# The gain of the first norm as one row, spread by TensorE, and transposes of the identity while the head waits

## The chip, the cores and the metric

The kernel runs on one core of a Trainium2 chip. The metric is the device time of one execution in microseconds; the median of several runs counts. The engines are PE (TensorE, matrix products and transposes), DVE (VectorE), ACT (ScalarE), POOL (GpSimd) and SP (SyncE, which here issues all the loads and stores). Each engine works through its own queue in order, and waits on semaphores for the others.

## What is computed

One step of a hybrid encoder layer on 1024 prompt rows and 32 sample rows of width 1024, all in f32: an RMS norm, one input projection whose columns feed window attention and a gated MLP over positions, an output projection with a residual, a second RMS norm with a SwiGLU of inner width 2816, a residual, and a last RMS norm. The part that matters here is the start:

```python
def rms_norm(x, g, eps=1e-6):
    xf = x.astype(jnp.float32)
    y = xf * lax.rsqrt(jnp.mean(xf * xf, axis=-1, keepdims=True) + eps)
    return (y * g.astype(jnp.float32)).astype(x.dtype)
...
        hp = rms_norm(yp, g_mix[l])
        q, k, v, u, g = project(hp, w_in[l])
```

`g_mix` is a vector of 1024 values, the gain of the first norm; every row of x is multiplied by it, element by element.

## The kernel before

The 1056 rows are nine tiles: eight of 128 rows and one of 32 (the sample). The head turns each tile into the form that the projection reads. `norm_front(r)` is shared by three engines: ACT squares the tile and sums it along the row (line 1530), POOL makes the root (lines 955 and 958), and DVE multiplies the tile by that root and by the gain in one instruction, `scalar_tensor_tensor` (line 1925), into `xn`. `norm_back(r)` follows: PE transposes `xn` in eight blocks of 128x128 against the identity `ident` into two banks of PSUM (line 1145), ACT rounds the result to the high part of `h_first`, `h_mid` or `h_late` (line 1537), and DVE subtracts it from the unrounded values for the low part (line 1905, the helper `low`). `split(n)` does the same with a 128-column unit of weights, ACT on line 1547 and DVE in `low`. `proj_block(n, half)` then multiplies: for each of eight k it makes three products (`three_passes`, lines 1108 to 1110) of 384 columns (288 for the last three tiles); a half is four k, twelve products. The first block needs the low parts of tiles 0, 1 and 2 and the first unit of weights.

The order of all this is written out by hand. `make_schedule()` gives one list, and PE, ACT, DVE and POOL each walk through it and do what concerns them:

```python
    s = [("front", 0), ("front", 1), ("back", 0), ("front", 2), ("split", 0), ("back", 1),
         ("front", 3), ("back", 2), ("split", 1), ("front", 4), ("back", 3), ("front", 5),
         ("block", 0, 0), ("back", 4), ("front", 6), ("block", 0, 1), ("back", 5), ("front", 7),
```

SP issues the loads in an order of its own (line 662 on): tile 0, the gain, tiles 1 and 2, the first weights. The gain is read from HBM 128 times, once for each partition:

```python
            load_rows(0)
            sp.dma_start(gain[:, :], a["g_mix"][0].partition_broadcast(P)).then_inc(gain_landed, 16)
            load_rows(1)
            load_rows(2)
```

The same tile `gain` later holds `g_ffn` and `g_final`, loaded in the same way. PSUM has eight banks of 128x512 f32, `ps[:, 0..7, :]`: the projection goes round banks 0 to 3, the transposes of the head use banks 4 to 7. POOL makes the constants at the start (lines 936 to 943), the identity last; `pool_consts` counts them. `one_row` is a row of ones on one partition, used by the attention for a mask.

Of the kernel before, what the change touches and what calls it, by code (L numbers as in the profile page):

```python
# [11 lines left out]
P = 128  # L12
# [252 lines left out]
def build(nc, a, o):  # L265
# [3 lines left out]
    with ExitStack() as ctx:  # L269
# [35 lines left out]
        one_row = sb("one_row", [1, DH])  # L305
# [117 lines left out]
        gain_landed = sem("gain_landed")  # L423
        wsp_landed = sem("wsp_landed")
# [189 lines left out]
        def _(sp):  # L614
# [46 lines left out]

            load_rows(0)
            sp.dma_start(gain[:, :], a["g_mix"][0].partition_broadcast(P)).then_inc(gain_landed, 16)
# [437 lines left out]
        def _(pe):  # L1101
# [23 lines left out]

            def norm_back(r):

                i = tile_of(r)
                rows, n = row_parts(i), (P if i != SAMPLE else DEC)
                pe.wait_ge(xn_ready, r + 1)  # L1130
                if r == 0:
                    pe.wait_ge(pool_consts, 6)
                if 2 <= r < ROWS:
                    pe.wait_ge(lo_ready, r - 1)
                if r == ROWS:
                    pe.wait_ge(attn_ready, UNITS)
                if r >= ROWS + 2:

                    pe.wait_ge(plain_lo, r - ROWS - 1)
                    if (r - ROWS) % 2 == 1:  # L1140
                        pe.wait_ge(t_2_ready, (r - ROWS) // 2)
                out = turned_pair(r)
                src = xn[rows, i % 2, :] if r < ROWS else xn_ffn[rows, :]
                for k in range(KT):
                    t = turn(out[:, k, 0:n], src[:, P * k:P * k + P], ident[rows, rows])  # L1145
                t.then_inc(turned, 1)

            def proj_block(n, half):
                t, b = PROJ_BLOCKS[n]
                if half != 1:  # L1150
                    if b == 0:
                        pe.wait_ge(split_lo, PLACE[t] + 1)
# [61 lines left out]
            def scores(u):  # L1214
# [7 lines left out]
                for x, i in enumerate(rows):  # L1222
                    for h in range(2):
# [13 lines left out]
                        if i == 0:  # L1237
                            mm(out[0:DH, at + DH:at + P], neg_row[:, :], one_row[:, :], start=True, stop=True)
                        else:
                            mm(out[0:DH, at + DH:at + P], q, k_t[hp, even - DH:even], start=True, stop=True)  # L1240
# [71 lines left out]

            for item in SCHEDULE:
# [186 lines left out]
        def _(act):  # L1500
# [31 lines left out]

            def norm_back(r):
# [71 lines left out]
            for item in SCHEDULE:  # L1605
# [3 lines left out]
                elif kind == "back":  # L1609
                    norm_back(item[1])  # L1610
                elif kind == "split":
# [291 lines left out]
        def _(dve):  # L1903
# [12 lines left out]
            def norm_front(r):  # L1916
# [4 lines left out]
                if r % ROWS == 0:  # L1921
# [4 lines left out]
                                               in1=gain[rows, :], op0=ALU.mult,  # L1926
# [511 lines left out]
```

## Time and profile before

| | us |
|---|---|
| median of 3 runs | 1028.12 (1028.02 to 1028.37) |
| the profiled execution | 1028.31 |
| its span | 1026.6 |
| PE busy | 1004.0 (98%) |
| DVE busy | 626.5 (61%) |
| ACT busy | 389.2 (38%) |
| POOL busy | 411.8 (40%) |

The span runs from the first to the last instruction that the profiler saw; 1.7 us of the execution's time lie around it. PE's share of busy time is close to the whole, but its products overlap by design, so their busy time doesn't tell how fast they follow each other: for that one reads the starts. All times in the rows below count from the start of the span.

### The profile page before, as it was taken

The numbers are of one execution on the slowest core, as the hardware profiler recorded it, in microseconds if no ns is written. First come the engines' busy times: TensorE is split into PE (matmuls) and PEld (weight loads), VectorE is DVE, ScalarE is ACT, GpSimd is POOL, SyncE is SP. The second block draws the span as 40 slices with busy tenths as digits, with TensorE's granted clock in tenths as the row PEclk, the third lists the DMA queues.
The fourth block names the chain that finished last, engine by engine and source line by source line (L and its number), as shares of the span: only waits on it lengthen the run. The fifth ranks groups of instructions, "written<-read, shape, count | busy, mean of one in ns | idle before, by whom it ended". The sixth has DMA issues, their size and how long they took to land.

```text
span 1026.6 us, 16280 instructions
## 1 busy us (share of the span) xinstructions
PE 1004.0 (98%) x5754; PEld 835.9 (81%) x5754; DVE 626.5 (61%) x877; ACT 389.2 (38%) x701; POOL 411.8 (40%) x444
## 2 busy tenths in 40 slices
PE   5999999999999999999999999999999999999997
PEld 4999998888887887787787787877878777877786
DVE  5475636766245786676766667666764737635725
ACT  6411145445232543333333333333333446324431
POOL 2011100000000467696696786876974400202045
PEclk9999999999999999999999999999999999999999
DMA  8311331100321444453643643644637999478814
GB/s 281 100 45 43 85 86 43 43 2 1 123 103 67 149 113 145 146 178 108 180 151 113 194 148 108 203 134 135 184 109 230 307 343 387 173 283 311 307 41 169
DMA packets 166274, 155.84 MB, mean 152 GB/s; under 512 B 16240, under 2 KB 129296, under 8 KB 166224
## 3 DMA queue, kind: packets, MB, share of 16 engines
q1 hardware_dynamic: 166224, 155.16, 47.0%
q8 instruction: 33, 0.54, 0.2%
q14 instruction: 17, 0.14, 0.0%
HBM read 114.17 MB, written 41.06 MB: 151 GB/s over the span
## 4 chain that ended last, share of the span: by engine, by line
PE 85%; DMA 6%; DVE 5%; SPq 1%; ACT 1%; issue 1%; POOL 0%; POOLq 0%; DVEq 0%; ACTq 0%
PE ps L1108 26%; PE ps L1110 25%; PE ps L1109 25%; DMA xd_in<-act_scratch 3%; PE ps L1394 2%; PE ps L1145 1%; DMA act_scratch<-act_sums 1%; PE ps L1280 1%; PE ps L1258 1%; DMA out_state_gmlp_v_sample<-work 1%; DVE x_dn L1905 1%; PE ps L1242 1%; DMA act_scratch<-ffn_blocks_even 1%; DVE work L1990 1%; PE ps L1482 1%
## 5 line engine op out<-in xcount | busy, mean ns | idle before, releaser
L1108 PE MATMUL ps<-x_forms,w_forms 128*128 128x512 f32 (+1 forms) x644 | 246.2, 382 | 0.7 <-DVE w_forms L1905 0.7
L1109 PE MATMUL ps<-x_forms,w_forms 128*128 128x512 f32 (+1 forms) x644 | 244.7, 380 | 0.0
L1110 PE MATMUL ps<-x_forms,w_forms 128*128 128x512 f32 (+1 forms) x644 | 244.5, 380 | 0.0
L1108 PEld LDWEIGHTS ps<-x_forms,w_forms 128*128 128x128 f32 x644 | 121.1, 188 | 28.2 <-issue 4.7
L1110 PEld LDWEIGHTS ps<-x_forms,w_forms 128*128 128x128 f32 x644 | 121.1, 188 | 23.0
L1109 PEld LDWEIGHTS ps<-x_forms,w_forms 128*128 128x128 f32 x644 | 121.1, 188 | 22.6
L1108 PE MATMUL ps<-w_dn,x_dn 128*128 128x512 f32 x308 | 121.6, 395 | 1.1 <-DVE y_acc_sample L2368 1.1
L1110 PE MATMUL ps<-w_dn,x_dn 128*128 128x512 f32 x308 | 119.9, 389 | 0.0
L1109 PE MATMUL ps<-w_dn,x_dn 128*128 128x512 f32 x308 | 119.9, 389 | 0.0
L955 POOL TENSOR_SCALAR meansq<-sumsq 128x1 f32<-128x1 f32 (+1 forms) x26 | 9.5, 365 | 246.3 <-ACT xn_ffn L1530 223.1
L1689 ACT CAST w_forms<-w_sums 128x512 fp32r<-128x512 f32 x88 | 54.6, 623 | 109.9 <-PE ps L1110 104.2
L1905 DVE TENSOR_TENSOR w_dn<-wd_in,w_dn 128x1024 fp32r<-128x1024 f32 (+1 forms) x42 | 49.3, 1174 | 73.3 <-ACT w_dn L1820 72.0
L1905 DVE TENSOR_TENSOR w_forms<-w_sums,w_forms 128x512 fp32r<-128x512 f32 x88 | 72.0, 829 | 18.9 <-ACT w_forms L1689 18.8
L1108 PEld LDWEIGHTS ps<-w_dn,x_dn 128*128 128x128 f32 x308 | 57.8, 188 | 23.5 <-issue 6.7
L1820 ACT CAST w_dn<-wd_in 128x1024 fp32r<-128x1024 f32 (+1 forms) x42 | 41.1, 978 | 90.5 <-DMA wd_in<-in_w_down 42.0
L1110 PEld LDWEIGHTS ps<-w_dn,x_dn 128*128 128x128 f32 x308 | 57.8, 188 | 12.2
L1109 PEld LDWEIGHTS ps<-w_dn,x_dn 128*128 128x128 f32 x308 | 57.8, 188 | 11.6
L1905 DVE TENSOR_TENSOR x_dn<-xd_in,x_dn 128x1024 fp32r<-128x1024 f32 (+1 forms) x42 | 51.7, 1230 | 6.4 <-ACT x_dn L1833 4.4
L1069 POOL TENSOR_TENSOR y_acc_even<-resid,down_u 128x512 f32<-128x512 f32 x4 | 6.2, 1560 | 106.0 <-DVE down_u L2345 78.3
L2212 DVE TENSOR_TENSOR ffn_q<-ffn_q 128x512 f32<-128x512 f32 (+1 forms) x23 | 19.8, 860 | 46.0 <-ACT ffn_q L1708 46.0
L1833 ACT CAST x_dn<-xd_in 128x1024 fp32r<-128x1024 f32 (+1 forms) x42 | 41.2, 980 | 11.7 <-DMA xd_in<-act_scratch 11.6
L1905 DVE TENSOR_TENSOR wbuf<-stage,wbuf 128x1024 fp32r<-128x1024 f32 x22 | 26.8, 1219 | 29.2 <-ACT wbuf L1547 29.2
(254 smaller groups left out, 2113.0 us busy)
## 6 DMA issues: line engine op xcount, KB each, us to landing
xd_in<-act_scratch SPq DMA_DIRECT2D x35, 512.0 KB, 7.3
t_raw<-in_w_down SPq DMA_DIRECT2D x88, 128.0 KB, 2.6
act_scratch<-act_sums SPq DMA_DIRECT2D x22, 512.0 KB, 4.5
y_acc_odd<-in_w_down SPq DMA_DIRECT2D x22, 512.0 KB, 6.4
wd_in<-t_scratch SPq DMA_DIRECT2D x20, 512.0 KB, 7.0
wd_in<-in_w_down SPq DMA_DIRECT2D x15, 512.0 KB, 6.5
stage<-in_w_in SPq DMA_DIRECT2D x28, 256.0 KB, 3.5
w_stage_even<-in_w_gate SPq DMA_DIRECT2D x22, 256.0 KB, 3.3
```

Source lines behind the costliest of these rows:

```text
L1108: mm(out, wh, xh, start=first, stop=False, skip_group_check=onto)
L1109: mm(out, wh, xl, start=False, stop=False, skip_group_check=onto)
L1110: return mm(out, wl, xh, start=False, stop=last, skip_group_check=onto)
L1145: t = turn(out[:, k, 0:n], src[:, P * k:P * k + P], ident[rows, rows])
L1242: last = mm(out[DH:P, at:at + P], cat[hp, j, odd:odd + DH], k_t[hp, even:even + P], start=True, stop=True)
L1258: t = turn(ps[:, 6, at:at + P], probs[:, u % 3, 2 * h + x, :], ident[:, :])
L1394: t = mm(out, x_sample[:, k, :], w_stage[q][:, :, k, :], start=k < 4, stop=k >= KT - 4)
L1689: nc.scalar.copy(wf[:, n, 0, :, :], src).then_inc(w_form_hi, 1)
L1820: nc.scalar.copy(w_dn[k % RING][:, 0, 0:pairs, :], wd_in[k % STAGED_FORMS][:, 0:pairs, :]).then_inc(w_dn_hi, 1)
L1833: nc.scalar.copy(x_dn[k % RING][:, 0, 0:pairs, :], xd_in[k % STAGED_FORMS][:, 0:pairs, :]).then_inc(x_dn_hi, 1)
L1905: return nc.vector.tensor_tensor(out, x, hi.bitcast(F32), ALU.subtract)
L2212: nc.vector.tensor_tensor(pq[:, 0, cols], pq[:, 0, cols], pq[:, 1, cols], ALU.add).then_inc(q_ready, 1)
```

## The change

The gain of the first norm is no longer loaded 128 times. SP loads it once, as its first load, into partition 0 of `gain`. PE, ahead of everything else in its queue, multiplies a row of ones (`one_row`, now 128 long) with it in two products of 512 columns (`spread_gain`), which leaves the gain on all partitions of PSUM banks 2 and 3. DVE's products of tiles 0, 1 and 2 read it there. After `norm_back(1)` ACT has a new step, `keep_gain`: it waits until DVE has made tile 2 and copies the gain from PSUM into `gain`, from where DVE reads it from tile 3 on. The block that goes to bank 2 first waits for that copy.

Besides, PE transposes the identity into bank 1, with no reader (`idle_turns`): 14 times before `norm_back(0)`, 8 times each before `norm_back(1)` and `norm_back(2)`, in each case ahead of the wait for the tile, and 6 times before the first block, ahead of its waits.

```diff
-        one_row = sb("one_row", [1, DH])
+        one_row = sb("one_row", [1, P])
...
+            sp.dma_start(gain[0:1, :], a["g_mix"][0:1, :]).then_inc(gain_landed, 16)
             load_rows(0)
-            sp.dma_start(gain[:, :], a["g_mix"][0].partition_broadcast(P)).then_inc(gain_landed, 16)
             load_rows(1)
...
+            def spread_gain():
+
+                pe.wait_ge(pool_consts, 6)
+                pe.wait_ge(gain_landed, 16)
+                for h in range(2):
+                    t = mm(ps[:, 2 + h, :], one_row[:, :], gain[0:1, 512 * h:512 * h + 512], start=True, stop=True)
+                t.then_inc(gain_spread, 1)
+
+            def idle_turns(n):
+
+                for _ in range(n):
+                    turn(ps[:, 1, 0:P], ident[:, :], ident[:, :])
...
             def norm_back(r):
...
+                if r < 3:
+                    idle_turns([14, 8, 8][r])
                 pe.wait_ge(xn_ready, r + 1)
-                if r == 0:
-                    pe.wait_ge(pool_consts, 6)
...
             def proj_block(n, half):
                 t, b = PROJ_BLOCKS[n]
                 if half != 1:
+                    if n == 0:
+                        idle_turns(6)
+                    if n == 2:
+                        pe.wait_ge(gain_kept, 1)
...
+            spread_gain()
             for item in SCHEDULE:
...
+            def keep_gain():
+                act.wait_ge(xn_ready, 3)
+                nc.scalar.copy(gain[:, :], ps[:, 2:4, :].rearrange("p b c -> p (b c)")).then_inc(gain_kept, 1)
...
                     norm_back(item[1])
+                    if item[1] == 1:
+                        keep_gain()
...
-                if r % ROWS == 0:
+                g = gain[rows, :]
+                if r == 0:
+                    dve.wait_ge(gain_spread, 1)
+                if r < 3:
+                    g = ps[:, 2:4, :].rearrange("p b c -> p (b c)")
+                elif r == 3:
+                    dve.wait_ge(gain_kept, 1)
+                elif r % ROWS == 0:
                     dve.wait_ge(gain_landed, 16 * (r // ROWS + 1))
...
-                                               in1=gain[rows, :], op0=ALU.mult,
+                                               in1=g, op0=ALU.mult,
```

PE's queue at its start, before: the transposes of four tiles (32 of 128x128), then the first products of the projection.

```order
1 L1145 MATMUL ps<-ident,work 128x128 x32
2 L1108 MATMUL ps<-h_first,wbuf 128x384
3 L1109 MATMUL ps<-h_first,wbuf 128x384
4 L1110 MATMUL ps<-h_first,wbuf 128x384
5 L1108 MATMUL ps<-h_first,wbuf 128x384
```

The same place in the changed kernel: line 1133 is `spread_gain`, line 1139 the transposes of the identity, line 1160 those of the tiles, lines 1110 to 1112 the products of the projection.

```order
1 L1133 MATMUL ps<-gain,one_row 128x512 x2
2 L1139 MATMUL ps<-ident 128x128 x14
3 L1160 MATMUL ps<-ident,work 128x128 x8
4 L1139 MATMUL ps<-ident 128x128 x8
5 L1160 MATMUL ps<-ident,work 128x128 x8
6 L1139 MATMUL ps<-ident 128x128 x8
7 L1160 MATMUL ps<-ident,work 128x128 x16
8 L1139 MATMUL ps<-ident 128x128 x6
9 L1110 MATMUL ps<-h_first,wbuf 128x384
```

Tiles 2 and 3 follow each other with nothing between them, and the last six stand behind tile 3.

ACT's queue at its start, before: the squares (line 1530), the casts of tiles 0, 1, 2 (line 1537) and of weights (line 1547).

```order
2 L1530 ACTIVATE work,sumsq<-work 128x1024 x2
3 L1537 CAST h_first<-ps 128x8x128
4 L1530 ACTIVATE work,sumsq<-work 128x1024
5 L1547 CAST wbuf<-stage 128x1024
6 L1537 CAST h_first<-ps 128x8x128
7 L1530 ACTIVATE work,sumsq<-work 128x1024
8 L1537 CAST h_first<-ps 128x8x128
```

And in the changed kernel, where squares are on line 1550, casts on lines 1561 and 1571, and the copy of the gain on line 1555.

```order
2 L1550 ACTIVATE work,sumsq<-work 128x1024 x2
3 L1561 CAST h_first<-ps 128x8x128
4 L1550 ACTIVATE work,sumsq<-work 128x1024
5 L1571 CAST wbuf<-stage 128x1024
6 L1561 CAST h_first<-ps 128x8x128
7 L1555 COPY gain<-ps 128x1024
8 L1550 ACTIVATE work,sumsq<-work 128x1024
9 L1561 CAST h_first<-ps 128x8x128
```

The copy stands between the cast of tile 1 and the square of tile 3.

## Rows read from the trace of the kernel before

**Rows 1.** The page: the span, and each engine's busy time, share and instructions.

```profile
span 1026.6 us, 16280 instructions
...
PE 1004.0 (98%) x5754; PEld 835.9 (81%) x5754; DVE 626.5 (61%) x877; ACT 389.2 (38%) x701; POOL 411.8 (40%) x444
```

**Rows 2.** Waits of PE over the whole span: total us, times, longest us.

```profile
PE ps L1145 <- DVE work L1925: 11.9, 4, 7.9
PE ps L1255 <- DVE work L2068: 1.3, 1, 1.3
```

**Rows 3.** Chain that ended last, its first microseconds: start us, us, what.

```profile
0.81 0.39 SPq L660
1.25 5.30 DMA gain<-in_g_mix
```

**Rows 4.** PE's timeline of the head: start us, us, engine, line, op, out<-in, shapes.

```profile
7.92 1.97 PE L1145 MATMUL ps<-ident,work 128*128 128x128 f32 x8 [7.92 <-DVE work L1925]
...
17.83 1.97 PE L1145 MATMUL ps<-ident,work 128*128 128x128 f32 x8 [1.52 <-DVE work L1925]
19.45 0.67 PE L1108 MATMUL ps<-h_first,wbuf 128*128 128x384 f32 x1
19.91 0.52 PE L1109 MATMUL ps<-h_first,wbuf 128*128 128x384 f32 x1
20.23 0.52 PE L1110 MATMUL ps<-h_first,wbuf 128*128 128x384 f32 x1
...
22.85 1.03 PE L1145 MATMUL ps<-ident,work 128*128 128x128 f32 x8
23.64 0.42 PE L1108 MATMUL ps<-h_first,wbuf 128*128 128x384 f32 x1
...
25.14 0.33 PE L1110 MATMUL ps<-h_first,wbuf 128*128 128x384 f32 x1
...
26.63 0.42 PE L1108 MATMUL ps<-h_first,wbuf 128*128 128x384 f32 x1
...
28.80 1.03 PE L1145 MATMUL ps<-ident,work 128*128 128x128 f32 x8
```

**Rows 5.** Engines' busy time by stretch; behind POOL the granted clock, DMA share, GB/s.

```profile
15.00:20.00 5.00, 3.48 (x17) 3.08 (x16) 5.00 (x5) 3.65 (x7) 2.88 (x4) 1.00 1.08 366
```

**Rows 6.** DMA issues between 0 and 45 us: count, KB each, median us to landing.

```profile
gain<-in_g_mix SPq DMA_DIRECT2D x1, 512.0 KB, 5.3
...
work<-in_x_sample SPq DMA_DIRECT2D x1, 128.0 KB, 2.5
...
sink<-in_attn_sinks SPq DMA_DIRECT2D x1, 4.0 KB, 4.8
```

**Rows 7.** ACT's timeline of the head, columns as in rows 4.

```profile
4.15 1.06 ACT L1530 ACTIVATE work<-work 128x1024 f32<-128x1024 f32 x1 [2.07 <-DMA work<-in_x_prompt]
...
9.93 1.01 ACT L1537 CAST h_first<-ps 128x1024 fp32r<-128x1024 f32 x1 [0.89 <-PE ps L1145]
10.84 1.06 ACT L1530 ACTIVATE work<-work 128x1024 f32<-128x1024 f32 x1
...
14.32 1.06 ACT L1530 ACTIVATE work<-work 128x1024 f32<-128x1024 f32 x1
...
23.93 1.02 ACT L1537 CAST h_mid<-ps 128x1024 fp32r<-128x1024 f32 x1 [2.03 <-PE ps L1145]
```

**Rows 8.** DVE's timeline of the head, columns as in rows 4.

```profile
6.58 1.29 DVE L1925 SCALAR_TENSOR_TENSOR work<-work,rstd,gain 128x1024 f32<-128x1024 f32 x1 [5.52 <-DMA gain<-in_g_mix]
...
11.27 1.22 DVE L1905 TENSOR_TENSOR h_first<-ps,h_first 128x1024 fp32r<-128x1024 f32 x1
13.00 1.28 DVE L1925 SCALAR_TENSOR_TENSOR work<-work,rstd,gain 128x1024 f32<-128x1024 f32 x1 [0.52 <-POOL rstd L958]
...
16.49 1.28 DVE L1925 SCALAR_TENSOR_TENSOR work<-work,rstd,gain 128x1024 f32<-128x1024 f32 x1
```

**Rows 9.** Line 1482, plain f32 products of 512 columns: duration ns min/median/max.

```profile
L1482 PE MATMUL ps<-y_acc_odd,sample_in x88: 592/605/617, 815.9 to 951.2; 128*32 128x512 f32 x88
```

More of the change, by code:

```diff
@@ L423, in build @@
         gain_landed = sem("gain_landed")
+        gain_spread = sem("gain_spread")
+        gain_kept = sem("gain_kept")
         wsp_landed = sem("wsp_landed")
@@ L1237, in scores @@
                         if i == 0:
-                            mm(out[0:DH, at + DH:at + P], neg_row[:, :], one_row[:, :], start=True, stop=True)
+                            mm(out[0:DH, at + DH:at + P], neg_row[:, :], one_row[:, 0:DH], start=True, stop=True)
                         else:
```

## The prediction

> **What bounds the kernel now.** I read the page first: PE is busy for 1004.0 of a span of 1026.6 us [rows 1], so only what makes PE start earlier, or makes its work shorter, can move the end. The second view is what PE waited for: 11.9 of its idle 22.6 us are four waits in the head, each for the normalised rows of one tile, and the first alone is 7.9 us [rows 2]. The third is the chain that ended last, in its first microseconds: the issue of tile 0, then the transfer of the gain (5.30 us) [rows 3]. The fourth is PE's own timeline of the head [rows 4]: eight transposes step from 17.83 to 19.45, that is 0.20 us each, and later from 22.85 to 23.64 in the same form, or 0.10 each. The products of 384 columns take 0.52 at first and 0.33 later; their starts step by 0.32, and twelve of them later by 0.18 (26.63 to 28.80). 384 columns in 0.32 us are 1.2 GHz, and 0.18 us with the end of the transposes in it belongs to 2.4 GHz. Twelve steps from 19.45 to 22.85 (3.40 us) are about nine of 0.32 and three of 0.18. So the whole head runs at the lower of the two levels until about 22.3, though the granted clock of its stretch is printed as 1.00 [rows 5]: the level has to be read from durations here. It rises 4.5 us after PE began to work without a pause at 17.83. From 22.85 PE hardly pauses (its longest wait behind the head is 1.3 us [rows 2]), so what PE is early at `norm_back(4)`, the transposes at 22.85, it is early at the end.
>
> **The change part by part.**
>
> **The gain's transfer.** Before, it takes 5.3 us to land and stands ahead of tile 1 in SP's queue [rows 6]. Without the 512 KB the later loads land some 2 us earlier, but only two waits of the head ended with a load: the gain itself (DVE started 0.3 us later than the root of tile 0 allowed: 4.15 + 2.16 = 6.3, against 6.58) and ACT's square of tile 1, after which ACT still idled 0.89 us for PE before the first cast [rows 7, 8]. The new row of 4 KB is issued first, so that tile 0 is issued 0.44 us later (0.81 to 1.25, the step between two issues [rows 3]) and lands at 4.6 instead of 4.1. From its square to DVE's product are 2.16 us (10.84 to 13.00, and 2.17 from 14.32 to 16.49) [rows 7, 8], from DVE's product to PE 1.34. So tile 0 reaches PE at 4.6 + 2.16 + 1.34 = 8.1, where it was 7.92: 0.2 later, not earlier.
>
> **The spreading product.** The row's landing is not in the trace. The nearest row is a load of 128 KB with nothing ahead of it, 2.5 us [rows 6]; so at most 0.81 + 2.5 = 3.3, and I take 3.1. The two products have 512 columns of plain f32, 605 ns for one at the high level [rows 9]. Two in a row at the low level cost between 1.2 (if nothing doubled) and 2.4 us (if all did); I take 1.9, since the fixed part doesn't double. The gain stands in the bank by 5.0 to 5.7, before DVE asks for it at 6.8: hidden by tile 0's square and root, with 1.1 us to spare.
>
> **The first 14 turns** start at 5.0 and take 2.8 us at 0.20 each: until 7.8, just before tile 0 is there at 8.1. They cost nothing on the path, at either level. PE is by then at work since 3.1. With the 4.5 us that the rise took before, the level rises at 7.6; I allow 6.5 to 10 and take 8.3.
>
> **norm_back(0).** At the high level the cast behind it starts 1.08 after its first transpose (22.85 to 23.93), at the low one 2.01 (7.92 to 9.93) [rows 4, 7]. With the rise at 8.3: 8.1 + 1.08 + 0.1 = 9.3, a gain of 0.6. ACT's next steps follow in order: square of tile 2 at 10.2, DVE's product at 12.4 (was 13.00), its result at 13.7.
>
> **The copy of the gain (`keep_gain`)** is new on ACT and waits for that third product. Behind it in ACT's queue stand the square of tile 3, the cast of tile 2, and through them everything up to the first projection. ACT would have gone on at 13.2; now it copies at 13.75 and is free at 14.7 (0.91 to the next instruction, as after a cast of 128x1024, 9.93 to 10.84). The square of tile 3 starts at 14.7, where it was 14.32; DVE's product of tile 3 at 16.85, where it was 16.49; tile 3 reaches PE at 18.2, where it was 17.83. The copy thus gives back the whole 0.6 and 0.35 more. Bounds of this term: 0 if the copy ran beside something, 0.95 as costed. DVE's reading of the gain from PSUM I cost at nothing: its subtraction with an operand from PSUM takes 1.22 (11.27), the product from SBUF 1.28 (13.00) [rows 8].
>
> **The turns before norm_back(1), norm_back(2) and the first block.** The first eight end at 8.1 + 0.8 + 0.1 + 0.8 = 9.8, tile 1 is ready at 9.4: 0.4 late, hidden, since ACT casts tile 1 only at about 12.2. The second eight end at 11.4, 2.3 us before tile 2 is there. Then PE pauses twice, 11.4 to 13.7 and 14.6 to 18.2. The six turns stand after norm_back(3): 18.2 + 0.8 + 0.6 = 19.6, and the low part of tile 2 is ready on DVE at 18.05 + 1.2 = 19.25 (two steps of DVE behind 16.85), so the turns cost 0.35 there. The first block starts at 19.6, before at 19.45: 0.15 later.
>
> **The first block** takes 3.40 us before (19.45 to 22.85), and 2.17 at the high level (26.63 to 28.80) [rows 4]: 1.23 less, if the level has lasted through the pause. It ends at 21.8, was 22.85. Tile 4 must be there: DVE's product of it follows the low parts of tile 2 and of the second weights, 18.05 + 1.15 + 1.15 = 20.35, ready at 21.7: just in time.
>
> **The sum:** the head ends 22.85 - 21.8 = 1.1 us earlier, all of it from the block's clock. If the level rises before 7.6 the chain on ACT and DVE sets the end, and the gain is 1.4; if it rises only at 10, the cast of tile 0 is where it was, and 0.4 are left. The profiled execution took 1028.31 (span 1026.6), the median is 1028.12; from the median: **1027.0**, between 1026.7 and 1027.7.
>
> **The rivals.**
>
> **The level falls again in the pause before norm_back(3).** 3.6 us without any work (14.6 to 18.2) is longer than each pause between the transposes before (1.5 us at 17.83), and no row shows what the level does in a pause once it is high. Then norm_back(3) and the six turns run at the low level: the block starts at 18.2 + 1.6 + 1.2 = 21.0. If the rise takes 4.5 us from 18.2 again, at 22.7, then 0.85 us of work is still lost to it: 21.0 + 2.17 + 0.85 = 24.0, 1.2 later than before. If it falls only near the end of the pause and rises early, 0.1 is lost. 1028.2 to 1029.3, middle 1028.7.
>
> **Turns don't raise the level (slower).** For it: before, three groups of eight transposes (7.92 to 16.3) raised nothing, and the level rose only 2.9 us after the first real product. Against: their pauses of 1 to 1.5 us explain that as well, and at 17.83 the 4.5 us that preceded the rise began with transposes. Then all is at the low level: norm_back(0) 8.1 to 9.7, eight turns to 11.3, norm_back(1) to 12.9, eight turns to 14.5, norm_back(2) to 16.2, and the cast of tile 0 starts at 10.1 in place of 9.3, which the chain by ACT and DVE hands on to tile 3: 19.0 in place of 18.2; norm_back(3) and six turns to 21.8, 2.35 after the 19.45 of before, and the low stretch of products behind that is as long as before. 1030.5. From a rise 2 us after the turns' end on it is slower by over 0.2%.
>
> The Trainium skill has this rule on its page "TensorE: Matmul & The Clock Gate", Part 4: PE-mode transpose: a transpose doesn't count as work for the clock the way a product does. By it the time would be that of this rival; the trace has no row that decides.
>
> **The copy is not on the path.** If ACT's square of tile 3 didn't have to wait, DVE would come to tile 3 at 15.9 (12.4 and three steps), PE at 17.25, the block at 18.65: 0.8 earlier than before and 1.23 shorter, 1026.1, about on the bound of 0.2%. Against it stands the order of ACT's queue, in which the copy precedes that square.
>
> **Nothing moves.** The row lands late (4 KB for the sinks, behind other loads, took 4.8 us [rows 6], which would put the spread at 7.5), or other waits take what the block gives: within 0.3 of before, 1028.1.
>
> **How the numbers follow.** Forecast 0.52; level falls in the pause 0.17; turns don't raise it 0.14; copy off the path 0.08; nothing moves 0.09. A measurement here tells 0.2% (2.06 us) from no change. Faster by more: the larger half of the third rival, 0.05; slower by more: the second rival, 0.14; within: 0.81. The range leaves out the copy's rival and the second rival, and takes in the level's fall with its upper bound and a little beyond: 1026.4 to 1029.6.
>
> **What would show it.** Right: two 512-column products before 5.7; eight transposes in about 1.0 us at 8 to 9 us and at 18.2; a copy of the gain on ACT from about 13.7, and the next square directly behind it; 0.17 or 0.18 from product to product from the first on; norm_back(4) at about 21.8. Wrong: norm_back(3) in 2 us (the level fell, or never rose; the transposes of tiles 1 and 2 say which), or a gain of over 1.5 us, which the chain by ACT excludes.

## The result, and the profile after

The changed kernel takes 1030.41 us (median of 13 runs, 1029.36 to 1034.78), the kernel before 1028.34 us in the same comparison (13 runs, 1027.33 to 1031.73). The ratio is 1.0021, with a 95% interval of 1.0011 to 1.0031: **2.1 us slower**, where 1.1 us faster was forecast, and above the upper end of the range. The profiled execution took 1029.77 us.

The page of the changed kernel, its span and busy times, beside [rows 1]: the span is 1.5 us longer, and PE is busy for 5.5 us more.

```profile
span 1028.1 us, 16363 instructions
...
PE 1009.5 (98%) x5794; PEld 839.8 (82%) x5794; DVE 628.8 (61%) x877; ACT 390.1 (38%) x702; POOL 407.6 (40%) x444
```

The waits of PE for DVE's tiles (total us, times, longest) are where [rows 2] had 11.9 us in four: six microseconds have gone, but the longest is now 3.8 us and stands before tile 3, not before tile 0.

```profile
PE ps L1160 <- DVE work L1958: 5.7, 2, 3.8
PE ps L1133 <- DMA gain<-in_g_mix: 2.3, 1, 2.3
```

PE's timeline of the head answers to [rows 4]. Line 1133 is the spreading product, 1139 the transposes of the identity, 1160 those of the tiles, 1110 to 1112 the projection.

```profile
2.32 3.75 PE L1133 MATMUL ps<-gain,one_row 1*128 1x512 f32 x4 [2.32 <-DMA gain<-in_g_mix]
6.00 3.11 PE L1139 MATMUL ps<-ident 128*128 128x128 f32 x14
8.95 1.04 PE L1160 MATMUL ps<-ident,work 128*128 128x128 f32 x8
9.82 1.04 PE L1139 MATMUL ps<-ident 128*128 128x128 f32 x8
...
14.44 1.09 PE L1160 MATMUL ps<-ident,work 128*128 128x128 f32 x8 [1.83 <-DVE work L1958]
19.37 1.97 PE L1160 MATMUL ps<-ident,work 128*128 128x128 f32 x8 [3.83 <-DVE work L1958]
21.13 1.49 PE L1139 MATMUL ps<-ident 128*128 128x128 f32 x6
22.27 0.53 PE L1110 MATMUL ps<-h_first,wbuf 128*128 128x384 f32 x1
22.63 0.34 PE L1111 MATMUL ps<-h_first,wbuf 128*128 128x384 f32 x1
...
24.54 1.04 PE L1160 MATMUL ps<-ident,work 128*128 128x128 f32 x8
```

Three things are to be seen. The first tile's transposes take 1.04 us instead of 1.97: the level of TensorE's clock (1.2 or 2.4 GHz, "the level" from here on) had risen by 8.95. After a pause of 3.83 us the eight transposes of tile 3 take 1.97 again: it had fallen. And `norm_back(4)`, the point that the sum was made for, starts at 24.54, where it was 22.85: 1.7 us later. The granted clock by stretch (the third number from the end, as in [rows 5]) shows the fall itself, which [rows 5] could not: from the first rise on the column follows the level.

```profile
14.50:15.50 1.00, 1.00 (x8) 0.79 (x8) 1.00 (x2) 1.00 (x2) 0.00 (x0) 1.00 1.04 332
15.50:16.50 1.00, 0.03 (x1) 0.00 (x0) 1.00 (x2) 1.00 (x3) 0.00 (x0) 0.58 1.26 324
21.00:22.00 1.00, 1.00 (x7) 1.00 (x6) 1.00 (x2) 0.63 (x1) 0.00 (x0) 0.50 0.90 356
22.00:23.00 1.00, 1.00 (x7) 1.00 (x6) 1.00 (x2) 1.00 (x2) 0.00 (x0) 0.75 0.01 0
```

0.58 over a microsecond is 0.16 us at 1.00 and the rest at 0.50: the level fell at about 15.7, some 0.15 us after `norm_back(2)` had ended, and rose again at about 22.5. This is the one profiled execution; of the 12 others the record has the mean granted clock alone, which was 0.996 or less in each.

ACT's and DVE's timelines of the changed kernel answer to [rows 7] and [rows 8]; in ACT's, line 1555 is the copy of the gain.

```profile
4.57 1.06 ACT L1550 ACTIVATE work<-work 128x1024 f32<-128x1024 f32 x1 [2.48 <-DMA work<-in_x_prompt]
...
10.02 1.01 ACT L1561 CAST h_first<-ps 128x1024 fp32r<-128x1024 f32 x1 [3.06 <-PE ps L1160]
...
14.42 1.01 ACT L1555 COPY gain<-ps 128x1024 f32<-128x1024 f32 x1 [0.49 <-DVE work L1958]
15.33 1.06 ACT L1550 ACTIVATE work<-work 128x1024 f32<-128x1024 f32 x1
```

DVE's products of tiles 2 and 3 in the changed kernel:

```profile
13.11 1.28 DVE L1958 SCALAR_TENSOR_TENSOR work<-work,rstd,ps 128x1024 f32<-128x1024 f32 x1 [0.81 <-POOL rstd L960]
...
17.57 1.75 DVE L1958 SCALAR_TENSOR_TENSOR work<-work,rstd,gain 128x1024 f32<-128x1024 f32 x1 [0.91 <-POOL rstd L960]
```

Behind the head the shift is carried on: the transposes of the spatial weights start at 54.0 (52.4 before), the first sample product of the output projection at 329.4 (328.2).

### The profile page after: what moved, and what is told of

Its sections match the earlier page's. It is cut to its first block, busy times and chain, and to the rows that moved or that the text cites. A ratio compares the mean times of both kernels' runs of the same rounds, so it can differ in the third digit from the quotient of the medians.

```text
span 1028.1 us, 16363 instructions
## 1 busy us (share of the span) xinstructions
PE 1009.5 (98%) x5794; PEld 839.8 (82%) x5794; DVE 628.8 (61%) x877; ACT 390.1 (38%) x702; POOL 407.6 (40%) x444
## 4 chain that ended last, share of the span: by engine, by line
PE 93%; DMA 3%; DVE 2%; ACT 1%; issue 1%; SPq 0%; POOL 0%; POOLq 0%; DVEq 0%; ACTq 0%
PE ps L1110 28%; PE ps L1112 27%; PE ps L1111 27%; DMA xd_in<-act_scratch 3%; PE ps L1414 2%; PE ps L1160 1%; PE ps L1299 1%; PE ps L1277 1%; PE ps L1229 1%; PE ps L1502 1%; PE ps L1261 1%; PE ps L1218 0%; PE ps L1255 0%; PE ps L1139 0%; PE ps L1133 0%
## 5 line engine op out<-in xcount | busy, mean ns | idle before, releaser
L1111 PEld LDWEIGHTS ps<-x_forms,w_forms 128*128 128x128 f32 x644 | 121.1, 188 | 22.5
L1111 PEld LDWEIGHTS ps<-w_dn,x_dn 128*128 128x128 f32 x308 | 57.8, 188 | 11.6
L2245 DVE TENSOR_TENSOR ffn_q<-ffn_q 128x512 f32<-128x512 f32 (+1 forms) x23 | 20.8, 903 | 45.6 <-ACT ffn_q L1734 45.6
```

Source lines behind the costliest of these rows:

```text
L1111: mm(out, wh, xl, start=False, stop=False, skip_group_check=onto)
L2245: nc.vector.tensor_tensor(pq[:, 0, cols], pq[:, 0, cols], pq[:, 1, cols], ALU.add).then_inc(q_ready, 1)
```

## The experiments

The time of this kernel scatters. Part of it comes from one place far behind the head: around 866 us PE waits for DVE's `y_acc_sample`, at the end of a chain of loads. In the kernel before, the chain that ended last reads there (start us, us, what):

```profile
813.99 10.69 DMA act_scratch<-act_sums
...
828.02 8.15 DMA xd_in<-act_scratch
...
841.47 10.57 DMA xd_in<-act_scratch
...
854.39 7.12 DMA xd_in<-act_scratch
...
865.91 0.70 DVE y_acc_sample L2368
866.66 0.50 PE ps L1108
```

The wait of PE at its end was 1.1 us in this run and 0.3 to 2.4 us in the others. So each experiment is read at two places: in the head of its trace, where differences of 0.1 us can be seen, and in the ratio to the kernel before, whose interval is 1.0 to 1.7 us to each side. In the head one more thing differs from run to run: tile 0 landed between 4.15 and 5.23 us. The table has its landing as the start of ACT's first square. The last column counts the runs whose mean granted clock over the span was 0.997 or less, which I take for at least one fall of the level on record; in the kernel before these are 18 of 110 runs, with a median of 1032.1 us against 1028.4 of the others. The column doesn't say where the level fell. In the kept profiles with such a mean the fall lies in the head for the changed kernel, e1, e3, e9 and e11, and near 866 us, behind that wait, for e5, e10 and e12.

The times are starts in us.

| kernel | square of tile 0 | cast of tile 0 | transposes of tile 3 | first product | norm_back(4) | ratio (interval) | runs at 0.997 or less |
|---|---|---|---|---|---|---|---|
| before | 4.15 | 9.93 | 17.83 | 19.45 | 22.85 | 1 | 18 of 110 |
| changed | 4.57 | 10.02 | 19.37 | 22.27 | 24.54 | 1.0021 (1.0011 to 1.0031) | 13 of 13 |
| e1 row only | 5.03 | 10.55 | 19.89 | 21.50 | 24.41 | 1.0009 (0.9997 to 1.0021) | 7 of 10 |
| e2 turns only | 4.74 | 10.27 | 18.14 | 19.65 | 22.14 | 0.9994 (0.9978 to 1.0010) | 5 of 10 |
| e3 copy late | 4.88 | 10.90 | 18.77 | 21.67 | 24.97 | 1.0008 (0.9997 to 1.0020) | 10 of 10 |
| e4 second pause filled | 5.07 | 11.14 | 20.48 | 21.98 | 24.17 | 1.0013 (1.0001 to 1.0025) | 2 of 10 |
| e5 copy late, all filled | 4.75 | 10.28 | 18.15 | 19.37 | 22.13 | 1.0011 (0.9994 to 1.0027) | 8 of 12 |
| e6 old load, all filled | 4.62 | 9.27 | 17.39 | 18.61 | 20.85 | 0.9988 (0.9974 to 1.0002) | 5 of 12 |
| e7 as e5, 14 turns | 5.23 | 10.74 | 18.61 | 19.84 | 22.61 | 1.0006 (0.9993 to 1.0019) | 0 of 12 |
| e8 as e5, copy early | 4.87 | 10.40 | 20.63 | 21.43 | 23.60 | 1.0005 (0.9990 to 1.0020) | 3 of 12 |
| e9 first pause filled | 4.85 | 11.06 | 20.41 | 22.32 | 25.68 | 1.0023 (1.0007 to 1.0039) | 9 of 12 |
| e10 as e6, 10 turns | 4.65 | 9.30 | 17.54 | 18.77 | 21.01 | 0.9989 (0.9975 to 1.0002) | 4 of 12 |
| e11 fewer turns | 4.70 | 10.22 | 19.56 | 21.18 | 25.17 | 1.0020 (1.0003 to 1.0036) | 10 of 12 |
| e12 e6 again | 4.80 | 9.45 | 17.54 | 18.77 | 21.01 | 0.9986 (0.9974 to 0.9997) | 4 of 12 |

**The theory that the experiments test.** The level does fall while PE waits for tiles 2 and 3 (the first rival of the prediction), the pause before tile 3 is made longer by the copy on ACT, and the turns and the product stand on the path besides. **The rivals.** The turns alone do the harm; or the gain's new way alone does it, whatever the level.

### The two halves apart (e1, e2)

e1 is the changed kernel without its transposes of the identity:

```diff
-                if r < 3:
-                    idle_turns([14, 8, 8][r])
...
-                    if n == 0:
-                        idle_turns(6)
```

> The changed kernel without any of its 36 transposes of the identity: the gain comes as one row, is spread by the product, and is copied by ACT behind tile 2. Theory (the gain's half of the change costs time by itself, since the copy stands ahead of ACT's square of tile 3): tile 3 reaches PE at about 19.4 as in the changed kernel (17.83 before), its eight transposes and most of the first block run at the low level, norm_back(4) starts at about 24.0, where it was 22.85: 1.1 us slower than before. Rival (the copy is free, all of the loss comes from the turns): tile 3 at 17.9, norm_back(4) at 22.9, no change to before.

Measured: `norm_back(4)` at 24.41, with tile 0 later by 0.9 than in the kernel before and by 0.5 than in the changed one. That all of the loss comes from the turns is out: without a single turn the head is longer by 1.6 us, of which at most 0.9 is tile 0's landing, and tile 3 reaches PE at 19.89. The ratio is 1.0009, between that of the kernel before and that of the changed one, and its interval takes in 1. Beside the gain's new way the turns don't pay either: e1 reaches `norm_back(4)` 0.13 earlier than the changed kernel does with them, though its tile 0 landed later.

e2 is the kernel before with the turns alone:

```diff
+                if r < 3:
+                    idle_turns([14, 8, 8][r])
                 pe.wait_ge(xn_ready, r + 1)
...
+                    if n == 0:
+                        idle_turns(6)
```

> The kernel before, with the gain loaded 128 times as it was, and only the transposes of the identity added (14, 8, 8 and 6 at the same places). Theory (turns raise the level, and without the copy the pause before norm_back(3) is about 1.5 to 2 us, too short for the level to fall): the level is high from norm_back(1) or (2) on, the first block starts at 19.2 to 19.5 and takes 2.2 us, norm_back(4) at 21.4 to 21.8 in place of 22.85: 1.1 to 1.4 us faster than before. Rival (the level doesn't hold through a pause of even 1.5 us): norm_back(3) in 1.6, six turns in 1.2, first block from 20.7, norm_back(4) at about 23.5: 0.6 slower than before.

Measured: `norm_back(4)` at 22.14, 0.7 earlier than before though tile 0 landed 0.6 later; the level was high from 13.4 on and held through a pause of 2.37 us in this profile:

```profile
18.14 1.09 PE L1152 MATMUL ps<-ident,work 128*128 128x128 f32 x8 [2.37 <-DVE work L1934]
```

The gain is less than the 1.1 to 1.4 that were expected, and tile 0's landing is enough to explain that; the ratio, 0.9994, can't be told from 1. In the head, then, the turns alone help and the way of the gain costs; in the time neither half can be told from no change.

### The pauses and the level (e3, e4, e9)

e3 is the changed kernel with the copy behind `norm_back(4)`:

```diff
             def keep_gain():
-                act.wait_ge(xn_ready, 3)
+                act.wait_ge(xn_ready, 6)
...
-                    if item[1] == 1:
+                    if item[1] == 4:
                         keep_gain()
...
-                if r < 3:
+                if r < 6:
                     g = ps[:, 2:4, :].rearrange("p b c -> p (b c)")
-                elif r == 3:
+                elif r == 6:
                     dve.wait_ge(gain_kept, 1)
```

> The changed kernel with the copy of the gain moved on ACT from behind norm_back(1) to behind norm_back(4), and DVE reading the gain from PSUM for tiles 0 to 5. Theory (the copy ahead of the square of tile 3 makes the pause in which the level falls): the square of tile 3 starts at 13.8 in place of 15.3, tile 3 reaches PE at about 18.0 in place of 19.37, the pause is 2.4 us and the level holds; the first block starts at 19.4 at the high level, norm_back(4) at 21.6: 2.9 us faster than the changed kernel and 1.2 faster than before. Rival (the level falls in a pause of 2.4 us too): norm_back(3) at 18.0 takes 1.6, the turns 1.2, the block starts at 20.8, norm_back(4) at 23.1 to 23.9: 0.6 to 1.4 faster than the changed kernel, at best even with the one before.

The pause before tile 3 came down from 3.83 to 2.37 us, as expected; the level fell all the same, at 17.3, and stayed down until 24.1. The granted clock by stretch of e3 (third number from the end):

```profile
16.50:17.50 1.00, 0.00 (x0) 0.00 (x0) 1.00 (x2) 1.00 (x2) 0.84 (x2) 0.89 1.08 345
23.50:24.50 1.00, 1.00 (x6) 1.00 (x5) 0.98 (x2) 0.00 (x0) 0.32 (x1) 0.70 0.71 188
```

PE's timeline of the same stretch of e3:

```profile
15.31 1.09 PE L1160 MATMUL ps<-ident,work 128*128 128x128 f32 x8 [1.83 <-DVE work L1958]
18.77 1.97 PE L1160 MATMUL ps<-ident,work 128*128 128x128 f32 x8 [2.37 <-DVE work L1958]
20.53 1.49 PE L1139 MATMUL ps<-ident 128*128 128x128 f32 x6
```

The theory's number fails here, and the rival's reading (the level can fall around a pause of 2.4 us) holds: e2 had the same pause of 2.37 us in its profile and kept the level, e3 lost it, and all 10 runs of e3 have a low mean clock. Five of the 10 runs of e2 have one too, against 18 of 110 before, so that such a pause alone may be enough at times. What e3 has and e2 has not is another pause, of 1.83 us, shortly before.

e4 is the changed kernel with its second pause filled:

```diff
-                if r < 3:
-                    idle_turns([14, 8, 8][r])
+                if r < 4:
+                    idle_turns([14, 8, 8, 30][r])
```

> The changed kernel with 30 more transposes of the identity ahead of the wait of norm_back(3), so that PE works through its longest pause (3.83 us). The copy stays where it is. Theory (the level falls in that pause, and its fall costs 0.9 us in norm_back(3) and 0.6 in the six turns): tile 3 still comes at 19.4, norm_back(3) takes 0.8, the turns 0.6, the block starts at 20.8 in place of 22.27, norm_back(4) at 23.0 in place of 24.54: 1.5 us faster than the changed kernel, about 0.1 slower than before. Rival (the level doesn't follow from the pause): norm_back(3) again in 1.8 us, no change to the changed kernel.

PE's timeline of e4 around its pauses:

```profile
15.55 1.09 PE L1160 MATMUL ps<-ident,work 128*128 128x128 f32 x8 [1.83 <-DVE work L1958]
16.48 3.44 PE L1139 MATMUL ps<-ident 128*128 128x128 f32 x30
20.48 1.09 PE L1160 MATMUL ps<-ident,work 128*128 128x128 f32 x8 [0.56 <-DVE work L1958]
21.41 0.82 PE L1139 MATMUL ps<-ident 128*128 128x128 f32 x6
```

Tile 3 takes 1.09 in place of 1.97 and the six turns 0.82 in place of 1.49, though tile 3 came 1.1 later than in the changed kernel (tile 0 landed 0.5 later and the level rose later). Only 2 of 10 runs recorded a fall, in place of 13 of 13. The level falls for the pauses: shown, by the count above all. `norm_back(4)` is only 0.4 earlier than in the changed kernel. The time gained against it, 0.8 us by the medians, has the right sign and is smaller than the 1.5 expected; the two intervals overlap, so the gain in time is not shown.

e9 is the changed kernel with its first pause filled:

```diff
-                    idle_turns([14, 8, 8][r])
+                    idle_turns([14, 8, 24][r])
```

> The changed kernel with 24 in place of 8 turns before norm_back(2), so that PE works through the first of its two pauses (1.83 us before norm_back(2)) and keeps the second (3.83 us before norm_back(3)): the counterpart of e4, which filled the second alone. In the changed kernel's trace the level fell 0.2 us after the second pause began. Theory A (it was the first pause and the thin work behind it that let it fall): the level holds longer, falls later in the second pause or not at all, norm_back(3) or the turns behind it are faster, norm_back(4) at 23.0 to 24.0 in place of 24.54. Theory B (the long pause alone is enough): the fall comes within that pause in each run, recorded clock 0.996 and below, norm_back(4) at 24.4 or later.

PE's timeline of e9 from tile 3 on:

```profile
20.41 1.09 PE L1160 MATMUL ps<-ident,work 128*128 128x128 f32 x8 [3.84 <-DVE work L1958]
21.33 1.34 PE L1139 MATMUL ps<-ident 128*128 128x128 f32 x6
```

With the first pause gone, tile 3 was still transposed at the high level (1.09 us, behind 3.84 us of pause), and the level fell at about 21.5, during the six turns. It stayed low until 24.9, through most of the first block, and `norm_back(4)` came at 25.68; 1.0 of the 1.1 us against the changed kernel was there already at the cast of tile 0, before which the level had not risen. Theory A said that the fall would come later, and is right in that; that this would help is wrong: 9 of 12 runs fell, and the ratio is 1.0023. The fall comes behind the pause as well as within it.

Put together: with both pauses the low mean clock is there in 13 of 13 and 10 of 10 runs (changed, e3), with the long one alone in 9 of 12 (e9), with the first one of 1.83 us alone in 2 of 10 (e4), about as often as before, and with none in 0 of 12 (e7, below). What decides between a fall and none at a given pause stays open.

### The price of the turns and of the copy (e5, e7, e8, e11)

e5 is e3 with the turns as long as the waits; e7 is e5 with 14 turns in place of the first 6:

```diff
-                if r < 3:
-                    idle_turns([14, 8, 8][r])
+                if r < 4:
+                    idle_turns([6, 0, 29, 22][r])
...
-                        idle_turns(6)
+                        idle_turns(0)
```

> The changed kernel with the copy behind norm_back(4) as in e3, and other numbers of transposes of the identity: 6 before norm_back(0), none before norm_back(1), 29 before norm_back(2), 22 before norm_back(3), none before the first block, so that PE pauses nowhere for more than about 0.5 us once it has begun. Theory (the level falls because of pauses while tiles are awaited, and the rest of the loss is the copy and the first 14 turns): tile 0 is transposed at 8.5, tile 3 at 18.1, all at the high level from 9 us on, the first block starts at 19.3, norm_back(4) at 21.6; 1.2 us faster than before, and the recorded clock stays at 0.998 or more. Rival (what the change costs lies elsewhere, the gain in PSUM or the spreading product): norm_back(4) at 23 or later, no faster than before.

PE's timeline of e5 in the head:

```profile
8.27 3.48 PE L1160 MATMUL ps<-ident,work 128*128 128x128 f32 x16 [0.71 <-DVE work L1958]
11.59 3.33 PE L1139 MATMUL ps<-ident 128*128 128x128 f32 x29
14.75 1.04 PE L1160 MATMUL ps<-ident,work 128*128 128x128 f32 x8
15.63 2.57 PE L1139 MATMUL ps<-ident 128*128 128x128 f32 x22
18.15 1.09 PE L1160 MATMUL ps<-ident,work 128*128 128x128 f32 x8
```

The head does what the theory said, from tile 3 on: 18.15, 19.37, 22.13, the last 0.7 earlier than before. But the level rose at about 11.5, not at 9, and the time is not shorter: 1.0011. Eight of 12 runs have a fall on record, and in the profile it is not in the head. PE's wait behind the loads was 2.4 us, and the granted clock fell right after it. The wait, from e5's waits (total us, times, longest):

```profile
PE ps L1110 <- DVE y_acc_sample L2401: 2.4, 1, 2.4
```

The eight microseconds behind it, in e5's busy time by stretch; the granted clock is 0.79:

```profile
868.00:876.00 8.00, 8.00 (x30) 6.40 (x29) 7.34 (x8) 6.05 (x6) 0.00 (x0) 0.79 1.03 376
```

So part of what the head gives can be lost 850 us later, to a fall behind a wait again. It isn't lost each time: e7 and e2 had the same wait (2.4 and 2.3 us) in their profiles and no fall. Whether a shorter head makes this wait longer stays open: it was 2.4 in e5 and e7 and 2.3 in e2 and e12, whose first product of line 1482 (1502, 1491) starts at 815.6, 816.2, 815.3 and 814.0 (815.9 before), and 0.3 and 0.4 in e3 and e1, which are late there (818.5 and 817.0), but 1.0 in e6, which is early at 814.3.

> As e5, but with 14 turns before norm_back(0) as in the change. Theory (at the low level 14 turns behind the spreading product end 0.9 us after tile 0 is there, and all of the head shifts with them): norm_back(0) at 9.2 to 9.4 in place of 8.5, norm_back(4) 0.7 to 0.9 later than in e5, the time as much longer. Rival (hidden, as the prediction had it): no difference to e5.

`norm_back(4)` came 0.48 after that of e5, and tile 0 had landed 0.48 later: no price for eight more turns in these two profiles. With 14 turns the level rose before the end of tile 0's transposes (16 of tiles 0 and 1 in 2.30 us, in place of 3.48), which paid for them. My figure of 0.7 to 0.9 doesn't hold. No run of e7 has a fall on record, its head is 0.2 shorter than before, and yet the ratio is 1.0006: PE went on behind the loads at 868.3 us, where it did at 866.7 before.

e8 is e5 with the copy behind `norm_back(1)`, as in the change:

```diff
-                    idle_turns([6, 0, 29, 22][r])
+                    idle_turns([6, 0, 29, 34][r])
```

> As e5, but with the copy behind norm_back(1) as in the change, and 34 turns before norm_back(3), so that the longer pause is filled. The level is held in both, so the difference is the price of the copy alone. Theory (it keeps the square of tile 3 waiting and makes DVE's product of tile 3 meet POOL's triangle): tile 3 at 19.1 to 19.4 in place of 18.1, norm_back(4) 1.2 us later than in e5. Rival (the copy fits in a pause of ACT): below 0.3 us.

DVE's product of tile 3 in the timeline of e8:

```profile
17.93 1.75 DVE L1958 SCALAR_TENSOR_TENSOR work<-work,rstd,gain 128x1024 f32<-128x1024 f32 x1 [0.91 <-POOL rstd L960]
```

The same in e5:

```profile
16.82 1.27 DVE L1958 SCALAR_TENSOR_TENSOR work<-work,rstd,ps 128x1024 f32<-128x1024 f32 x1
```

POOL's triangle beside it in e5:

```profile
16.59 0.64 POOL L972 TENSOR_SCALAR_AFFINE_SELECT work<-work 128x512 f32<-128x512 f32 x1
```

The product starts 1.1 later in e8 and takes 0.48 longer. POOL's triangle runs beside it in both (0.64 us at 17.97 in e8). What differs is where the product reads the gain: from `gain` in e8 (1.75 us), from PSUM in e5, e3 and e7 (1.27 each, beside the triangle all the same). So the early copy costs DVE these 0.5 us by taking the gain out of PSUM before tile 3. The price in the head is 1.1 on ACT and 0.5 on DVE: tile 3 is ready for PE at 19.7 in place of 18.1. `norm_back(4)` is at 23.60 in place of 22.13, and that 1.5 isn't the price of the copy alone, as I had meant it to be. The level rose only at about 13.9 in e8, so the 29 turns held up tile 2, and the 34 held up tile 3: PE came to it at 20.63, 0.9 after it was ready, without a wait. In the time no difference shows (1.0005 against 1.0011); 3 of 12 runs of e8 have a fall on record, 8 of 12 of e5.

e11 is the changed kernel with fewer turns:

```diff
-                    idle_turns([14, 8, 8][r])
+                    idle_turns([6, 8, 8][r])
...
-                        idle_turns(6)
+                        idle_turns(0)
```

> The changed kernel with the turns on the path taken out: 6 in place of 14 before norm_back(0), none in place of 6 before the first block; 8 and 8 stay, and so does the early copy. Theory (the turns stand in the way: 0.9 us before norm_back(0), up to 1.2 before the block at the low level; the copy and the fall of the level remain): norm_back(0) at 8.2, tile 3 at 18.9 to 19.4, the first block starts at 21.0 at the low level, norm_back(4) at 23.7 to 24.0 in place of 24.54: 0.6 to 0.8 faster than the changed kernel, still 1 slower than before. Rival (the turns keep the level up and their loss costs more than their place): norm_back(4) at 24.5 or later.

The first product did start earlier, at 21.18 in place of 22.27. But the level was low from 18.4 to about 25.2, so all of the first block ran at it, and `norm_back(4)` came at 25.17. The cast of tile 0 came no earlier with 6 turns than with 14 (10.22 against 10.02; tile 0 had landed 0.13 later): the eight turns won by their clock what they cost by their place. The rival holds; no gain, 1.0020.

### A version that beats both (e6, e10, e12)

e6 is e2 (the old load of the gain, no product, no copy) with the turns as long as the waits:

```diff
-                if r < 3:
-                    idle_turns([14, 8, 8][r])
+                if r < 4:
+                    idle_turns([28, 18, 12, 20][r])
...
-                        idle_turns(6)
+                        idle_turns(0)
```

> The kernel before with its 512 KB load of the gain, no spreading product, no copy, and turns that fill all pauses: 28 before norm_back(0), 18 before norm_back(1), 12 before norm_back(2), 20 before norm_back(3), none before the first block. Theory (only the turns are worth something, and only if no pause is left): the level is high from about 8 us, tile 3 is transposed at 17.3, the first block starts at 18.3, norm_back(4) at 20.8, 2.0 us earlier than before. If the level rises only at 12 or later, the 18 turns at 0.21 delay tile 1 by up to 2 us and nothing is won. Rival (the gain as one row is what helps, since the load of 512 KB delays tiles 1 and 2): slower than e5.

PE's timeline of e6 in the head:

```profile
1.84 6.10 PE L1129 MATMUL ps<-ident 128*128 128x128 f32 x28 [1.84 <-POOL ident L942]
8.13 1.10 PE L1152 MATMUL ps<-ident,work 128*128 128x128 f32 x8 [0.20 <-DVE work L1934]
...
17.39 1.09 PE L1152 MATMUL ps<-ident,work 128*128 128x128 f32 x8 [0.42 <-DVE work L1934]
...
20.85 1.09 PE L1152 MATMUL ps<-ident,work 128*128 128x128 f32 x8
```

`norm_back(4)` at 20.85, 2.0 us earlier than before, as worked out, though tile 0 landed 0.5 later. e10 has 10 in place of the 18 turns and gives the same.

> As e6 (the old load of the gain, no product, no copy; 28, 18, 12, 20 and 0 turns), but with 10 in place of 18 turns before norm_back(1). The rise of the level came between 6 and 12 us after PE's first work in the runs so far; where it is late, 18 turns delay tile 1 by up to 2 us and 10 by 0.5. Theory: norm_back(4) again at 20.8 to 21.0, 1.9 earlier than before, with fewer late runs than e6; median 1.0 to 2.0 below before. Rival: the pause of 1.3 us that is left before norm_back(1) puts the rise off, norm_back(4) at 22 or later, no gain.

> The kernel of e6 once more, to settle whether it beats the one before: e6 gave a ratio of 0.9988 with an interval that just touches 1. Theory (the head is 2.0 us shorter, and the stage that waits for loads near 866 us hands that on with its own scatter of about 1 us): a mean 1 to 2 us below before, ratio 0.998 to 0.999. Rival (what the head gives is lost to PE's wait in that stage): ratio 0.9995 to 1.0005.

0.9988, 0.9989 and 0.9986, the last with an interval below 1 (0.9974 to 0.9997): **about 1.3 us faster than the kernel before**, and 3.4 us faster than the changed one. The intervals of e6 and e10 just reach beyond 1; that the repeat, e12, says the same is what carries the claim. In e12 eight runs had no fall on record and took 1026.1 to 1027.1 us; the four others took 1028.4 to 1028.9. Of the 2.0 us of the head about two thirds arrive. At 815.9 us, the place of the first product of line 1482 before, e6, e10 and e12 are still 1.6 to 2.0 early; the kept profile of e12 is one of the four slower runs, and its level is low from about 866.2 to 869.6, behind the wait of 2.3 us.

## Why the prediction was wrong

Step by step, with the changed kernel's trace:

- **The transfer of the gain.** Right in this run: tile 0 landed 0.42 later (4.57 against 4.15), and no other load held up ACT or DVE in the head. The number was luck in part: e2, e6, e10 and e12 issue their loads as the kernel before does, and tile 0 landed at 4.62 to 4.80 in them.
- **The spreading product.** The step failed by its size. The row was there at 2.32, earlier than the 3.1 assumed, but the two products cost 3.68 us (2.32 to 6.00) and not 1.9, not even within the 1.2 to 2.4 taken as bounds: the trace has four records of 1.06 to 1.19 us for them, two for each product, 0.92 us from one to the next. [rows 9] give the duration of one record, and I took a record for a product.
- **The first 14 turns.** By that alone they start at 6.00 in place of 5.0, and end at 8.95, 0.85 after tile 0 was there at 8.1 (DVE's product from 6.76, and the 1.34 of the prediction). What was costed at nothing had lost its cover. The cast of tile 0 came at 10.02 in place of 9.3, 0.7 late.
- **The rise.** Right in this run (8.9 against 8.3), but by chance: its distance from PE's first work was 4.3 to 11.6 us over the other runs. In the kernel before the same distance is 14 us. The 4.5 us read from one burst in the trace of before is no figure to plan with.
- **The copy.** The mechanism was right and was predicted to 0.1: 14.42 to 15.33, and the square of tile 3 directly behind it. Behind the 0.7 that came from the turns, DVE's product of tile 3 starts at 17.57. The step left out its neighbour: POOL's triangle runs beside this product, as it did before; but before it was POOL's that took longer (1.68 in place of 0.64), and now it is DVE's (1.75 in place of 1.28).
- **The level in the pause.** This is the step that failed by its mechanism, and by the most: the sum of the forecast let the level last through the pause of 3.6 us and put its fall at nothing. I gave the fall 0.17 and the forecast 0.52. It fell in the profiled run, and the mean clocks of all 13 runs are as low as that one's or lower. It costs 0.95 in `norm_back(3)` (1.76 from start to start in place of 0.8) and 0.55 in the six turns (1.14 in place of 0.6).

The level was not all of it. Had it held, the first product would have come at 20.8 and `norm_back(4)` at about 23.0: no gain over the 22.85 of before, where 1.1 was forecast.

The sum closes: the first product starts at 22.27 in place of the 19.6 forecast; 0.7 (product and turns), 0.5 (DVE beside POOL) and 1.5 (the level) are 2.7. The first block at the high level took 2.27, as forecast (2.17), so that the change does win 1.1 us there and gives back 2.8 ahead of it: 1.7 later in all. The measured 2.1 agrees with that within its interval. That part of it is scatter behind the head is likely and not shown. Three of the 13 runs had a mean granted clock of 0.994 or less and took 1032.7 to 1034.8; the others had 0.995 or 0.996 and took 1029.4 to 1032.0.

The rival of the falling level was priced at 1028.2 to 1029.3, and its mechanism came true at 1030.4. It was mis-sized because it was worked out on top of the other terms as forecast, and two of these were wrong in the same direction. A third error hid 0.7 of that: the rival had the level rise 4.5 us after tile 3 came, and it rose 3.1 after (22.5 against 19.37). The second rival, that transposes don't raise the level, had nearly the measured number and is refuted: in e6 PE did nothing but 28 transposes of the identity, and tile 0 was then transposed in 1.10 us. By the Trainium skill's page "TensorE: Matmul & The Clock Gate", Part 4: PE-mode transpose, transposes don't count toward the clock like products do; in e6, e10 and e12 the level was high at 8.1 to 8.3 us with no product before it, so here the measurement decides against that sentence. The third rival (copy off the path) was rightly held unlikely.

The reading that would have helped stood in the rows: in a head with 11.9 us of waits in four pieces an early rise of the clock can be lost again before the products, until the pauses are closed. The kernel before ran no such risk: its level rose at about 22.2, with no pause behind it.

## What to carry to other kernels

Work that only keeps TensorE busy pays where it fills a wait whole, up to the moment when the data comes; put in pieces with pauses of 1.8 and 2.4 or 3.8 us behind them, it let the level rise early and fall again just before the products, in every run as far as the mean clocks tell (13 of the changed kernel, 10 of e3). Saving a transfer that is waited for by 0.3 us is worth no more than that, and the instructions that replace it (here two products of 3.7 us together and a copy on the engine that sets the pace) are cost. And what ends up on the path is counted from the engine's slowest level and its dearest form: if the trace has no record of an operation, its price is open in both directions, and a filler placed behind it loses its cover first.

## What was not expected of the hardware

- The fall comes at no fixed place in the long pause: it came 0.15 us into the pause of 3.83 in the changed kernel, 0.9 us into that of 2.37 in e3, and 1 us after a pause of 3.84 in e9. The low level then lasted 6.8 us in the changed kernel (15.7 to 22.5) and in e1 (16.3 to 23.1).
- The recorded granted clock is 1.00 before the first rise even where durations show the low level, as [rows 5] do, and follows the level only afterwards.
- A 4 KB load with nothing ahead of it could be used by PE 1.5 us after its issue began (0.81 to 2.32); in the other runs with this load PE started at 2.32 to 2.63.
- DVE's product of tile 3 and POOL's triangle over 128x512 cost one another time when they meet, if the product reads both tensors from SBUF: DVE took 1.75 us in place of 1.28 when it began at 17.57 and POOL at 17.60, and 1.49 to 1.56 in e6, e10 and e12, where POOL began 0.15 to 0.23 ahead. Before, POOL's took 1.68 us beside an undisturbed 1.28 of DVE. With the gain in PSUM neither was slower (e3, e5, e7: 1.27 and 0.64). POOL's row in the kernel before:

```profile
16.59 1.68 POOL L970 TENSOR_SCALAR_AFFINE_SELECT work<-work 128x512 f32<-128x512 f32 x1
```

And in the changed kernel:

```profile
17.60 0.64 POOL L972 TENSOR_SCALAR_AFFINE_SELECT work<-work 128x512 f32<-128x512 f32 x1
```
